# Leaving out the filling matmuls behind two post norms of a two-block transformer kernel

## The reference

```python
def token_mixer(x, g_pre, g_post, ..., w_out):
    h = rmsnorm(x, g_pre)
    ...
    return x + rmsnorm(merged @ w_out, g_post)

def channel_mixer(x, g_pre, g_post, w_gate, w_up, w_conv, b_conv, w_down):
    h = rmsnorm(x, g_pre)
    a = causal_dwconv(h @ w_gate, w_conv, b_conv)
    y = (jax.nn.gelu(a, approximate=True) * (h @ w_up)) @ w_down
    return x + rmsnorm(y, g_post)
```

## Time and profile before

| | us |
|---|---|
| median of 3 runs | 1443.18 (1442.7 to 1443.27) |
| the profiled execution | 1443.08 |
| its span, first to last instruction | 1441.2 |
| TensorE busy in it | 1419.8 |
| VectorE (DVE) busy | 843.4 |
| ScalarE (ACT) busy | 607.6 |
| GpSimd (POOL) busy | 304.0 |

### The profile page before, as it was taken

How to read it: one execution, slowest core, us unless ns; L and a number is a source line. 1 busy time by engine, 2 the same in 40 slices (tenths; PEclk the granted TensorE clock), 3 DMA queues, 4 the chain that set the end, 5 groups by cost and what they waited for, 6 DMA issues and landing times.

```text
span 1441.2 us, 23105 instructions
## 1 busy us (share of the span) xinstructions
PE 1419.8 (99%) x9119; PEld 1224.6 (85%) x9119; DVE 843.4 (59%) x1271; ACT 607.6 (42%) x926; POOL 304.0 (21%) x287
## 2 busy tenths in 40 slices
PE   8999999999999999999999999999999999999999
PEld 7999999999998988998997677767678888888887
DVE  6888654457465543553354737898877534344355
ACT  6552577743343231222224446666655314233230
POOL 2660334300115622660463000002103000000000
PEclk9999999999999999999999999999999999999999
DMA  5212112124312232233224132111133222323221
GB/s 207 72 63 83 51 59 74 59 89 148 103 60 80 96 117 88 88 102 103 88 87 140 54 104 71 59 42 47 52 118 116 98 98 90 102 92 106 93 95 66
DMA packets 35848, 128.34 MB, mean 89 GB/s; under 512 B 4084, under 2 KB 4468, under 8 KB 35632
## 3 DMA queue, kind: packets, MB, share of 16 engines
q1 hardware_dynamic: 34608, 122.18, 25.2%
q10 hardware_dynamic: 864, 4.33, 0.8%
q0 software_dynamic: 288, 0.57, 0.1%
HBM read 124.92 MB, written 2.10 MB: 88 GB/s over the span
## 4 chain that ended last, share of the span: by engine, by line
PE 85%; DVE 9%; POOL 2%; ACT 2%; issue 1%; DMA 0%; SPq 0%; DVEq 0%; ACTq 0%; POOLq 0%
PE ps L1967 70%; PE ps L2377 3%; DVE rot L980 2%; PE ps L2207 1%; POOL phase_tmp L1785 1%; PE ps L2473 1%; DVE w_lo L976 1%; PE ps L2496 1%; PE ps L2435 1%; DVE rot L1232 1%; PE ps L2486 1%; PE ps L2027 1%; POOL phase L1785 1%; PE ps L2319 1%; PE ps L2321 1%
## 5 line engine op out<-in xcount | busy, mean ns | idle before, releaser
L976 DVE TENSOR_TENSOR w_lo<-w_raw,w_hi 128x1024 fp32r<-128x1024 f32 (+2 forms) x225 | 294.2, 1309 | 146.0 <-ACT w_hi L392 145.7
L1967 PE MATMUL ps<-h_hi,w_hi 128*128 128x512 f32 (+3 forms) x1168 | 331.7, 333 | 3.9 <-DVE qk L980 1.8
L1967 PE MATMUL ps<-h_hi,w_lo 128*128 128x512 f32 (+3 forms) x1168 | 321.1, 324 | 0.0
L1967 PE MATMUL ps<-h_lo,w_hi 128*128 128x512 f32 (+3 forms) x1168 | 320.8, 324 | 0.0
L392 ACT ACTIVATE w_hi<-w_raw 128x1024 fp32r<-128x1024 f32 (+2 forms) x226 | 231.4, 1032 | 167.6 <-PE ps L1967 156.2
L1967 PEld LDWEIGHTS ps<-h_hi,w_hi 128*128 128x128 f32 x1168 | 196.1, 188 | 33.0 <-issue 11.7
L1967 PEld LDWEIGHTS ps<-h_lo,w_hi 128*128 128x128 f32 x1168 | 195.8, 188 | 19.9 <-issue 2.9
L1967 PEld LDWEIGHTS ps<-h_hi,w_lo 128*128 128x128 f32 x1168 | 195.8, 188 | 17.8
L1967 PE MATMUL ps<-f_hi,w_hi 128*128 128x256 f32 (+1 forms) x488 | 129.5, 319 | 0.0
L1967 PE MATMUL ps<-f_hi,w_lo 128*128 128x256 f32 (+1 forms) x488 | 129.5, 319 | 0.0
L1967 PE MATMUL ps<-f_lo,w_hi 128*128 128x256 f32 (+1 forms) x488 | 129.4, 319 | 0.0
(11 more groups left out here) (385 smaller groups left out, 2332.7 us busy)
## 6 DMA issues: line engine op xcount, KB each, us to landing
w_raw<-w_units SPq DMA_DIRECT2D x227, 512.0 KB, 3.2
x<-x_t ACTq DMA_DIRECT2D x1, 2112.0 KB, 8.1
out<-out_tile SPq DMA_DIRECT2D x7, 256.0 KB, 2.0
x<-x_t ACTq DMA_DIRECT2D x3, 528.0 KB, 9.0
x<-x_t ACTq DMA_DIRECT2D x2, 264.0 KB, 4.4
consts<-consts SPq DMA_DIRECT2D x1, 320.0 KB, 6.7
b_step<-ssm_b SPq DMA_DIRECT2D x1, 256.0 KB, 10.3
c_step<-ssm_c SPq DMA_DIRECT2D x1, 256.0 KB, 11.0
```

The source lines that it names most:

```text
L976: Dv.do(v.tensor_tensor(wlo[:, s % RING, 0:w], raw[:, s % RING, 0:w], f32(whi[:, s % RING, 0:w]), ALU.subtract), lo_ready)
L1967: ins = mm(o, wt[:, s % RING, w], xt[:, kx, c0:c0 + n], start=(b == 0 and a == 0), stop=(b == len(blocks) - 1 and a == 2))
```

## The change

The last parameter of `last_unit` goes, and with it the call of `keep_busy` behind the last sum of squares. Both callers drop their number, 14 and 6. All else stays: the order of the queues, the semaphores and the arithmetic of the outputs.

```diff
-            def last_unit(norm, n, s, xhi, xlo, outs, blocks, busy):
+            def last_unit(norm, n, s, xhi, xlo, outs, blocks):
 
                 j, h = POST.index(norm), n // 2
                 begin(s)
@@
                 unit(s, 0, xhi, xlo, outs[1:2], None, 0, blocks, after=first_sums)
                 pe.wait_ge(sem("sq_half"), 2 * j + 2)
                 mm(PS[:, 5, 0:h], ones, sq[1][:, h:n], start=False, stop=True).then_inc(sem("stat_mm"), 1)
-                keep_busy(ones, busy)
@@
             last_unit(1, TW, U_FFN - 1, hhi, hlo,
-                      [(PS[:, 2 * ((U_FFN - 1) % 2) + hf, 0:TH], T0 + TH * hf, TH) for hf in range(2)], [(k, k) for k in range(KT)], 14)
+                      [(PS[:, 2 * ((U_FFN - 1) % 2) + hf, 0:TH], T0 + TH * hf, TH) for hf in range(2)], [(k, k) for k in range(KT)])
@@
             last_unit(3, SEQ, U_V2 - 1, fahi, falo,
-                      [(PS[:, last + hf, 0:SEQ // 2], hf * SEQ // 2, SEQ // 2) for hf in range(2)], [(k, k) for k in range(tiles)], 6)
+                      [(PS[:, last + hf, 0:SEQ // 2], hf * SEQ // 2, SEQ // 2) for hf in range(2)], [(k, k) for k in range(tiles)])
```

## The result

Without the fillers the kernel takes 1445.53 us as the median of 20 runs (1443.74 to 1447.39), against 1443.07 us of 20 runs of before (1442.70 to 1444.45): ratio 1.0015, 95% interval [1.0009, 1.002]. It is slower by 2.5 us or 0.17%: the interval leaves out 1, so it is clear of noise, and it is still within the 0.2% that I had called the same. The profiled execution took 1446.14 us with a span of 1444.3 us, 3.1 us more than that of before.

A forecast was written before the change was run, and what follows sets the result against it. TensorE's stream was taken as the bound, except at the two pauses, bound by ACT and DVE chains. Fillers' time 0, first pause 1.65, second 0: 1443.08 + 1.65 = 1444.7 us, range 1442.7 to 1447.3.

The forecast's parts named there:

- The fillers' own time is worth nothing: At both pauses the ACT and DVE chain hides the fillers: removing their time gains 0, at most 0.13 us.
- the 0.03 to 0.13 that I gave: At the second pause the first useful matmul could come 0.03 to 0.13 us sooner; the path gains 0.
- They may hold up the clock: At the first pause, 3.57 us without fillers might let TensorE's clock fall to half; the trace can't tell.
- The price of a fall: After a pause, 4.3 us at 0.52 of the rate makes TensorE 2.05 us late, before cover by waits.
- I take 4.3: Length in us assumed for a slow stretch, taken from the one at the kernel's start (4.0 to 5.0).
- The cover at the first pause: TensorE's wait of 0.40 us for `f_lo` at 420.86, taken to absorb part of the 2.05 us loss.
- my 1.65: Net loss forecast at the first pause: 2.05 - 0.40 = 1.65 us, bounds 0 and 2.4 us.
- It reaches the end: Behind 421.6 us TensorE has no idle time to give back, so the 1.65 us stay.
- I take 0: Second pause: no loss, of 0 to 2.05 us possible, since its 1.09 us hole resembles holes at full clock.
- the forecast's own case, one fall: Clock falls at the first pause only: 1.65 us slower, 1444.7 us, chance 0.50.
- the fall at both pauses: Rival: clock falls at both pauses, the second uncovered; 3.70 us slower, 1446.8 us, chance 0.17.
- 1444.7: Forecast time of the whole kernel in us, with one clock fall at the first pause.

The follow-up runs named there:

- e1: Kernel before without the 14 filler calls at the first pause, the second keeping its 6: 1444.20 us, ratio 1.0004.
- e2: Kernel before without the 6 filler calls at the second pause, the first keeping its 14: 1444.86 us, ratio 1.0007.
- e12: Kernel before with fillers added around the second pause and at 113.6 us, but none at the first pause: 1443.64 us, ratio 1.0009.
- e3: Kernel before with 7 filler calls in place of 14 at the first pause: 1443.93 us, ratio 1.0.
- e11: Kernel before with fillers added around the second pause and at 113.6 us, but 7 calls for 14 at the first: 1443.00 us, ratio 1.0.
- e5: Kernel before with 6 more filler calls in TensorE's wait at 113.6 us: 1444.51 us, ratio 1.0004.
- e7: Kernel before with 28 filler calls in place of 14 at the first pause: 1444.88 us, ratio 1.0014.
- e8: Kernel before with its 14 and 6 filler calls moving 8 columns in place of 128: 1445.68 us, ratio 1.0017.
- e6: Kernel before with 9 more filler calls around the second pause and 6 more at 113.6 us: 1442.96 us, ratio 0.9997.
- e9: Second timing of the kernel before with 9 more filler calls around the second pause and 6 at 113.6 us: 1442.93 us, ratio 0.9998.
- e4: Kernel before with 9 more filler calls around the second pause: 1442.93 us, ratio 0.9997.

## Why the prediction was right or wrong

- **The fillers' own time is worth nothing**: right. At the first pause the useful work starts 4.27 us behind the last sum with and without them. At the second it starts 1.75 us behind it in place of 1.79, 0.04 us sooner, within the 0.03 to 0.13 that I gave, and the next wait swallowed it.
- **They may hold up the clock**: right, and no longer open: none of the 20 runs without fillers, and none of the 11 of e1, e2 and e12 each, has a clock of 1.000. The rule of the Trainium skill against long gaps ("TensorE: Matmul & The Clock Gate", section "Why this matters for your kernels") agrees with these runs at 3.57 us. It names long gaps alone, and the measurement here goes further: the clock also fell behind a hole of 2.01 us in e3 and e11, and behind one of 1.80 us in e3.
- **The price of a fall**: the rate was right, the length not. A pair of matmuls that followed at 0.23 us followed at 0.43, a rate of 0.54 where I took 0.52. The term that was mis-sized is "I take 4.3": the slow stretch at the start of the kernel was no measure for those behind a pause. They lasted 3.41 us (e1, e2, both of e3, e5, e7, e11, e12, and e8 at the second pause) or 6.83 us (both of the changed kernel, and e8 at the first pause). The cover at the first pause was mis-sized too, 0.64 us (e7) against 0.40. For a single fall at the first pause 1.65 us were forecast and 0.75 to 2.08 us measured in the traces. By the medians the first pause costs 1.0 us (e1) or 0.8 (e12), so my 1.65 was too high for the common case.
- **It reaches the end**: right. All of e7's 1.80 us did.
- **Behind the second pause "I take 0"**: this is the step that failed. No run of e2, where only this pause was opened, kept a clock of 1.000, and the fall there cost 0.6 us in the cheapest run (1443.53 against 1442.95), 1.04 us in the profiled run of the changed kernel and 1.66 us by e2's median. My reason was that holes of 1.2 and 1.37 us stood at full clock right beside it. That was a reading of one execution. In 34 of the 99 executions of the same kernel before whose clock is told it did fall, and e6 and e9, with both places filled, had one fall in 22: the places are the second pause, where e5's trace shows it with all fillers of before in place, and the wait at 113.6 us. The 1.000 of the earlier trace rows was one draw, and the step needed the spread of many.
- **The rivals**: the forecast's own case, one fall, was given 0.50 and the fall at both pauses 0.17. 14 of the 20 runs without fillers have a mean clock of 0.996 or less, which is 10.1 us or more at half clock, and one fall of 6.83 us doesn't make that. So more than one fall, as the rival has it, or one longer than any that was traced, was the common case; the one trace has two falls, one at each pause. Only two runs, at 1443.74 and 1444.21 us, have 0.999 and so a single short one. The rival's price was too high, 3.70 us against 3.06 in the profiled run and 2.46 between the medians. The 0.8 us by which I missed is the difference of two errors: e1 and e2 put the first pause at 1.00 us where I took 1.65, and the second at 1.66 where I took 0, and 1.00 + 1.66 = 2.66 us is near the 2.46 measured, each good to 1.3 us. That 1444.7 came out as near as it did owes something to luck.

What stays open: e3 was not able to tell whether half the filler is enough, and only e11 did; what makes a stretch 3.41 or 6.83 us long wasn't tried; and the runs with more than 6.83 us at half clock where only one pause was open (six of e2, two of e12, one of e1) have no trace.

## What to carry to other kernels

A filler that looks idle in the chain of waits may be holding the clock of the stretch behind it, so price its removal by what TensorE does next: here each microsecond at half clock under dense work cost 0.47 us (1.60 / 3.41). Read one clean profile as one draw: where the times of a kernel come in two groups and the mean clock goes with them, look for its sparse stretches first, since a hole of 1.2 to 2 us that is harmless in the trace at hand can be the upper group of the next. And fill a pause with full matmuls (128 or 512 columns kept the clock here, 8 did not) that end before its chain does: fillers that ran past it cost 1.80 of the 2.44 us that they ran over, all but the slack of the next wait.

## What was not expected of the hardware

- The clock fell while TensorE had records without a gap (e8: 1.90 of 1.90 us busy, then 0.50), when these moved 8 columns each; with 14 calls of 128 columns there is no fall at the first pause in any of the six traces that have them (before, e2, e4, e5, e6, e9). Here the busy share of the stretch didn't tell whether its clock would hold.
- The slow stretches have two lengths, 3.41 and 6.83 us, in all traces of this study, and begin at another place of the pause in every execution: at the first pause 2.17 (e8), 3.39 (the changed kernel), 3.93 (e12), 4.40 (e3), 4.50 (e1) and 5.33 us (e11) behind the start of the last sum.
- A filler on plain float32 with 512 columns takes 0.45 us a pass, where a record of the products with 512 columns takes 0.23 us from start to start; at 128 columns the filler takes 0.11.
